# Delta rule's inverse: levels up to 32 rows as 32x32 products of compact diagonal blocks, the last two levels on their non-zero blocks only

## The reference, cut to what matters

```python
def gdn_chunked(q, k, v, g, beta, s0):          # called for both directions
    gcum = jnp.cumsum(chunks(g), axis=-1)
    decay = jnp.where(tri, jnp.exp(gcum_i - gcum_j), 0.0)
    a_mat = jnp.where(strict, (kb @ k.T) * decay, 0.0)       # strictly lower
    t_inv = triangular_solve(eye + a_mat, eye)               # (I + A)^-1
    u, w = t_inv @ (vc * bc), t_inv @ (kb * exp(gcum))
    attn = (q @ k.T) * decay
    def step(state, xs):
        v_new = u_i - w_i @ state
        o_i = q_i @ state + a_i @ v_new
        state = state * exp(gl_i) + k_i.T @ v_new
```

## Time and profile before

| | |
|---|---|
| median of 3 runs | 3282.87 us (3281.56 to 3284.77) |
| the profiled execution | 3282.49 us; its span 3280.6 us |
| delta rule's six steps with lead-in and tail | 340.7 to 706.0 us of the span |
| granted PE clock over the span | 0.928 of 2.4 GHz |

### The profile page before, as it was taken

How to read it: one execution, slowest core, us unless ns; L and a number is a source line. 1 busy time by engine, 2 the same in 40 slices (tenths; PEclk the granted TensorE clock), 3 DMA queues, 4 the chain that set the end, 5 groups by cost and what they waited for, 6 DMA issues and landing times. The chain is left out here.

```text
span 3280.6 us, 39078 instructions
## 1 busy us (share of the span) xinstructions
PE 2813.6 (86%) x15829; PEld 1542.4 (47%) x15829; DVE 912.4 (28%) x1797; ACT 611.6 (19%) x1101; POOL 269.1 (8%) x209
## 2 busy tenths in 40 slices
PE   6998788886999999999889989985698878998993
PEld 4553788863433333444544444432245834444441
DVE  2720455533121121245651000000342554000002
ACT  4411221223101000123221110100232211101002
POOL 0100553421000000000120000000000011000001
PEclk8989899897999999999889999998799988999997
DMA  8122100033799999300147999996401304999996
GB/s 291 52 99 108 65 1 1 14 125 129 321 419 403 416 416 405 114 20 1 65 157 315 430 429 428 429 395 244 160 0 39 134 17 164 423 428 429 429 428 245
DMA packets 109506, 753.39 MB, mean 230 GB/s; under 512 B 20948, under 2 KB 24256, under 8 KB 70480
## 3 DMA queue, kind: packets, MB, share of 16 engines
q1 hardware_dynamic: 106224, 738.19, 54.9%
q0 software_dynamic: 2592, 12.58, 1.0%
q10 hardware_dynamic: 576, 1.05, 0.1%
HBM read 725.82 MB, written 25.97 MB: 229 GB/s over the span
## 5 line engine op out<-in xcount | busy, mean ns | idle before, releaser
L1691 PE MATMUL bank<-ring,expert_in 128*64 128x512 f32 x2048 | 471.4, 615 | 44.4 <-DMA ring<-in_moe_w_up_dram 42.1
L1691 PEld LDWEIGHTS bank<-ring,expert_in 128*64 128x64 f32 x2048 | 162.9, 141 | 346.3 <-issue 343.6
L1702 PE MATMUL bank<-ring,hidden_T 128*64 128x512 f32 x1024 | 226.8, 595 | 41.5 <-ACT hidden_T L1654 40.6
L1630 DVE TENSOR_TENSOR hidden<-silu_gate,bank 128x512 f32<-128x512 f32 x32 | 33.7, 1052 | 749.8 <-PE bank L1691 749.8
L1446 PE MATMUL bank<-ring,expert_in 128*64 128x512 f32 x1024 | 224.8, 597 | 6.5 <-DVE home L1294 5.5
L1680 PEld LDWEIGHTS bank<-onehot,x_part 128*128 128x128 bf16 x3072 | 176.2, 99 | 31.4 <-issue 24.3
L1680 PE MATMUL bank<-onehot,x_part 128*128 128x128 bf16 x3072 | 181.7, 222 | 6.8 <-DVE onehot L1621 6.8
L1702 PEld LDWEIGHTS bank<-ring,hidden_T 128*64 128x64 f32 x1024 | 72.1, 137 | 175.5 <-issue 149.1
L1446 PEld LDWEIGHTS bank<-ring,expert_in 128*64 128x64 f32 x1024 | 73.1, 138 | 156.0 <-issue 141.9
L2386 PE MATMUL bank<-ring,home 128*128 128x512 f32 x256 | 119.2, 628 | 21.6 <-PEq L189 21.6
L547 PE MATMUL bank<-home,ring 128*128 128x512 f32 (+1 forms) x384 | 127.8, 493 | 7.6 <-PEq L189 7.6
(11 more groups left out here) (586 smaller groups left out, 3682.2 us busy)
## 6 DMA issues: line engine op xcount, KB each, us to landing
ring<-in_moe_w_gate_dram SPq DMA_DIRECT2D x67, 2048.0 KB, 17.9
ring<-in_moe_w_up_dram SPq DMA_DIRECT2D x66, 2048.0 KB, 18.5
ring<-in_moe_w_down_dram SPq DMA_DIRECT2D x66, 2048.0 KB, 13.9
ring<-in_w_gate_dram SPq DMA_DIRECT2D x32, 2048.0 KB, 13.2
ring<-in_w_up_dram SPq DMA_DIRECT2D x32, 2048.0 KB, 14.6
ring<-in_w_down_dram SPq DMA_DIRECT2D x32, 2048.0 KB, 16.1
ring<-in_w_mod_dram SPq DMA_DIRECT2D x12, 2048.0 KB, 11.9
expert_rows<-expert_out SPq DMA_DIRECT2D x32, 512.0 KB, 17.4
```

Source lines behind the costliest of these rows:

```text
L1691: mm = pe.matmul(B[2 + 2 * part][rows, :], xe[:, c, rows], ws[e][:, c, :], start=(c == 0), stop=(c == NC - 1))
L1702: mm = pe.matmul(B[6 + b][rows, :], hT[:, c, rows], ws[e][:, c, b * COLS:(b + 1) * COLS], start=(c == 0), stop=(c == NF - 1))
```

## The change

U stays the full 128x128 tile, but for levels 0 to 4 the work is on compact tiles: `Uc`, `Vc`, `ACs`, `ALs`, `Qs` keep the four diagonal 32x32 blocks of each head side by side, 128 partitions by 4x32. A product of a level is then 16 matmuls of 32x32 (4 heads x 4 blocks, block b from partitions 32b to partitions 32b of the result), and the evictions and subtractions are 128x128 in place of 128x512. V is no longer made by a product: DVE transposes `Uc` in 32x32 blocks. All five masks of a step are applied by one POOL operation of 128x640 (`small_masked`), after ACT has cut the diagonal blocks out of A (`cut`, four operations per d). Level 5 multiplies only the 32x32 blocks below (above) the diagonal, level 6 only one 64x64 block per head. Off-diagonal results go straight into U; the diagonal blocks of U are copied there by DVE and ACT (`spread_half`, `spread_rest`). The work for step s+1 is dealt out by direction: one direction per level. `wT` and `vn` get tiles of their own, ring slot 5 holds the compact tiles, and on POOL `prepare` and the clearing of `oacc` come later. The loads on SP are the same.

```diff
+        masks, ALs, ACs = two_small(LS, SM), two_small(LS, HEADS, SM), two_small(HEADS, SM)
+        Uc, Vc, Vq, Qs = two_small(HEADS, SM), two_small(HEADS, SM), two_small(HEADS, 2 * SM), two_small(HEADS, 2 * SM)
...
             def _(pool):
-                pool.memset(oacc[:, :, :], 0.0).then_inc(zeroed, 1)
...
+                def small_masked(s, d):
+                    pool.wait_ge(cut_out, 2 * s + d + 1)
+                    if s:
+                        pool.wait_ge(q_done, step(s - 1, LS - 1, d) + 1)
+                    pool.tensor_tensor(ALs[d], ACs[d].unsqueeze(1).to_broadcast([P, LS, HEADS, SM]),
+                                       masks[d].unsqueeze(2).to_broadcast([P, LS, HEADS, SM]), ALU.mult).then_inc(al_ready, 1)
...
+                def part_of_inverse(s, L, d):
+                    if L == 1:
+                        pe.wait_ge(al_ready, 2 * s + d + 1)
+                    pe.wait_ge(inv_ready, made(s, L - 1, d) + 1)
+                    out = small_bank(d, 0, SM if L <= LS else 2 * SM)
+                    for h in range(HEADS):
+                        if L < LS:
+                            for b in range(P // SM):
+                                mm = pe.matmul(out[blk(b), h, :], ALs[d][blk(b), L, h, :], Uc[d][blk(b), h, :], start=True, stop=True)
+                        elif L == LS:
+                            for p in range(2):
+                                a, b = row_of(d, p), col_of(d, p)
+                                mm = pe.matmul(out[blk(a), h, :], AD[s % 2][d][blk(b), h, blk(a)], Uc[d][blk(b), h, :], start=True, stop=True)
                         else:
+                            a, b = quad(d), quad(1 - d)
+                            mm = pe.matmul(out[a, h, :], AD[s % 2][d][b, h, a], U[d][b, h, b], start=True, stop=True)
+                    mm.then_inc(q_done, 1)
...
+                    for L in range(1, LEVELS):
                         for d in range(2):
+                            part_of_inverse(s, L, d)
+                        if more and L <= 2:
+                            sums_of_gates(s + 1, L - 1)
+                        if more and L in (3, 4):
+                            with_keys(s + 1, L - 3, 4, kk_done)
+                        if more and L >= 5 and s + 1 >= NTC:
+                            with_keys(s + 1, L - 5, 0, qk_done)
+                        for d in range(2):
+                            into_inverse(s, L, d)
...
+                            keep_part(s, L, d)
+                        if L == LS:
+                            for d in range(2):
+                                spread_half(s, d)
+                        if L in (2, 3) and s + 1 < CHUNKS:
+                            exps(s + 1, L - 2)
...
+                    if L < LS:
+                        inv.then(dve.tensor_tensor(Uc[d], Uc[d], small_bank(d, 1), ALU.subtract))
+                        dve.transpose(Vc[d].rearrange("p h f -> p (h f)"), Uc[d].rearrange("p h f -> p (h f)")).then_inc(inv_ready, 1)
```

More of the change, by code:

```diff
@@ L824, in delta_net, with two_small @@
         sq = lambda t, h: idle[:, 14 * W4 + (HEADS * (t % 2) + h) * HD:][:, 0:HD]
+        small = m.ring[:, 5, :]
+        taken_small = [0]
+        def two_small(*shape):
+            size = int(np.prod(shape))
+            out = []
+            for d in range(2):
+                a = small[:, taken_small[0]:taken_small[0] + size]
+                taken_small[0] += size
+                out.append(a.rearrange("p (a b c) -> p a b c", a=shape[0], b=shape[1]) if len(shape) == 3 else a.rearrange("p (a b) -> p a b", a=shape[0]))
+            return out
@@ new lines, in with_keys @@
+                def with_keys(s, d, first, done):
+                    at = AT(chunk_of(s, d))
+                    if first == 4:
+                        pe.wait_ge(exp_ready, 2 * s + d + 1)
+                    else:
+                        pe.wait_ge(kk_taken, 2 * s + d + 1)
+                    for h in range(HEADS):
+                        mm = pe.matmul(pre(d)[:, h * P:(h + 1) * P], qkv[:, 4 + h, at:at + P], qkv[:, first + h, at:at + P],
+                                       start=True, stop=True)
+                    mm.then_inc(done, 1)
@@ new lines, in cut @@
+                def cut(s, d):
+                    act.wait_ge(ad_ready, 2 * s + d + 1)
+                    if s:
+                        act.wait_ge(al_ready, 2 * s + d - 1)
+                    for b in range(P // SM):
+                        ins = act.activation(ACs[d][blk(b), :, :], AD[s % 2][d][blk(b), :, blk(b)], ACT.Copy)
+                    ins.then_inc(cut_out, 1)
+                for d, first in enumerate(("lower0", "upper0")):
+                    at = CONST_NAMES.index(first)
+                    for b in range(P // SM):
+                        act.activation(masks[d][blk(b), :, :], m.const[blk(b), at:at + LS, blk(b)], ACT.Copy).then_inc(tables_made, 1)
@@ L1040, in _ @@
+                for b in range(P // SM):
+                    act.activation(ident[blk(b), :, :], m.c("ident")[blk(b), blk(b)].unsqueeze(1).to_broadcast([SM, HEADS, SM]), ACT.Copy).then_inc(tables_made, 1)
+                for d in range(2):
+                    exps(0, d)
+                for d in range(2):
+                    cut(0, d)
+                act.wait_ge(tables_made, 16)
                 for s in range(CHUNKS):
@@ L1059, in _ @@
                     for d in range(2):
                         act.wait_ge(vn_done, k0 + d + 1)
-                        act.activation(vn[d][:, :, :], bank3(d, 1), ACT.Copy).then_inc(vn_ready, 1)
+                        act.activation(vn[d][:, :, :], heads3(bank(d, 1)[:, :]), ACT.Copy).then_inc(vn_ready, 1)
+                    for d in range(2 if s + 1 < CHUNKS else 0):
+                        cut(s + 1, d)
                 for i, t in enumerate(outer_tiles):
                     act.wait_ge(o_added, i + 3)
-                    squares(t)
+                    for h in range(HEADS):
+                        square(t, h)
@@ L1111, in _ @@
+                for d in range(2):
+                    differences(0, d)
+                for d in range(2):
+                    weights_of_keys(0, d)
+                dve.wait_ge(tables_made, 16)
                 for s in range(CHUNKS):
                     k0 = 2 * s
+                    more = s + 1 < CHUNKS
                     for L in range(LEVELS):
@@ L1129, in _ @@
[L1129 to L1135 removed]
+                                first_level(s, d)
+                            else:
+                                next_level(s, L, d)
+                        if more and L in (1, 2):
+                            differences(s + 1, L - 1)
@@ new lines, in _ @@
+                        if more and L in (4, 5):
+                            weights_of_keys(s + 1, L - 4)
+                        if more and L == 6 and s + 1 >= NTC:
+                            for d in range(2):
+                                dve.wait_ge(ad_ready, 2 * (s + 1) + d + 1)
+                                weights_of_queries(s + 1, d)
+                    if s + 1 == CHUNKS:
+                        dve.wait_ge(o_rooted, 1)
+                        dve.reciprocal(rs[:, inner, :], ms[:, inner, :]).then_inc(o_inverse, 1)
@@ L1148, in _ @@
                                 so.then(ins)
-                        if s + 1 == CHUNKS:
+                        if not more:
                             continue
```

351 lines of the change are left out of this document (177 added, 174 removed).

## The result

| | before | after |
|---|---|---|
| median | 3283.82 us (4 runs, 3281.56 to 3288.28) | 3188.16 us (4 runs, 3185.76 to 3196.33) |
| ratio, 95% interval | | 0.9711 (0.969 to 0.9733) |
| profiled execution, its span | 3282.49, 3280.6 us | 3185.76, 3184.0 us |

What follows compares the result with a forecast made beforehand. PE's throughput, with a short wait over ACT and DVE, was taken to bound the stage. Gains of 14.4 + 19.8 + 67.8 + 20.1 less 0.5 made 121.6 us off 3282.5: 3161 against the median, range 3124 to 3208.

Steps and rivals of the forecast that it cites:

- Group of 16 products: Levels 1 to 4: 32 records of 32x32 products on PE take 0.45 us, 0.55 at half clock.
- fast bound: Lower limit for a group of 32 small records on PE: four blocks at once, 0.22 us.
- Full packing: Rival for the levels: group 0.22 us, clock stays at 2.4 GHz, levels on a 3.0 us floor; 3121 us, chance 0.2.
- slow bound: Upper limit for a group of 32 small records on PE: one record after the other, 0.86 us.
- second rival: Row tiles in the levels don't overlap, group 0.86 us, clock mostly half; 3206 us, chance 0.28.
- Level, 3.2 at full and 4.4 at half clock: Levels 1 to 4 with one direction's inserted work: 3.2 us at full clock, 4.4 at half, mean 3.8 taken.
- Transpose 0.25: In levels 1 to 4, DVE's transpose was taken as 0.25 us, nearest to the 0.22 us copy.
- Boundary 3.1: Between steps, DVE's state update and two small DVE operations: 3.1 us where 5.5 were, 3.6 in step 1.
- Clock 0.6 to 0.85: Granted clock in steps 2 to 4 going to and fro, between 0.6 and 0.85, not 0.92.
- Levels 5 and 6, 4.0 and 4.3: Level 5 with ACT evictions and DVE operations 4.0 us; level 6 with 64x64 products and queries waiting for DVE 4.3.
- Step 5's levels 2.7: Levels of the last step, with nothing inserted for a next step, take 2.7 us each.
- Step 0's stall: PE waits inside level 1 for POOL's `repeat(1)`, behind clearing and `prepare(0)` until 361.2; PE idle some 6 to 8 us.

Runs made afterwards that it cites:

- three edits: Changed kernel with POOL's second-step copies earlier, queries' products behind second halves of levels 5 and 6, first level's subtraction on POOL; together 3159.43 us.
- a fourth: On top of three edits: next gates' products between level 1's first groups, POOL copies ahead of masks, last diagonal copies ahead of the square root; 3167.63 us.

## Why the prediction was right, and where it was off

The sign and the range held, and so did the main mechanism: PE's large products were the bound, and it fell away with them. The sum was 25 us short against the profiled execution (27 by the medians), 22.1 of them in the stage (265.8 against 243.7) and the rest outside it, which is within what executions differ by. Nearly half of the 22 comes from levels 5 and 6, and some from a wait for instructions, a term that the prediction did not have. That it came so near is in part luck: groups that were faster than forecast made up for terms that were too small.

| | before | forecast | measured |
|---|---|---|---|
| lead-in and step 0 | 62.7 | 48.3 | 53.3 |
| step 1 | 55.7 | 35.9 | 39.0 |
| steps 2 to 4 together | 184.2 | 116.4 | 127.0 |
| step 5 to W | 42.8 | 21.2 | 24.4 |
| tail | 19.9 | 21.4 | 22.1 |

- **Group of 16 products, 0.45 us at the full clock and 0.55 at half:** measured 0.26 and 0.42, near the fast bound. Full packing was right and its rival 3121 still wrong. Of the 11 us a step that it misses in steps 2 to 4, 5.4 lie in levels 5 and 6 and 4.1 in levels 1 to 4: those at the full clock do take 3.2, near its 3.0, but those at half clock or with a gap don't. The Trainium skill's rule on one PSUM bank (TensorEngine Tiling (Array Packing), Restrictions and Gotchas) did not hold this group back: four row tiles wrote the bank at 7 ns spacing. The slow bound, 0.86 us, has its like in another order of the same products, 0.64 to 0.72 us at the full clock and 1.0 at half; that kernel takes 3236, where the second rival said 3206.
- **Level, 3.2 at full and 4.4 at half clock, 3.8 taken:** 3.2 to 3.5 and 4.4 to 5.1; four levels of step 2 took 14.9 us where 15.2 were taken. Right in size, by terms that made up for each other. A group takes 0.26, not 0.45, but the second direction comes 0.52 us after the first, behind DVE's subtraction and transpose, and the inserted products take 1.09 us (441.16 to 442.25), not 0.89. From there on PE's order is the way, as forecast.
- **Transpose 0.25:** 0.311 over 48, next to the subtraction's 0.274. The small ACT copies took 0.27 to 0.31 where 0.2 was taken.
- **Boundary 3.1 (3.6 in step 1), and 1.5 more on the wide products:** 3.0 into step 3 (473.77 to 476.72) and 2.9 into steps 4 and 5, but 3.8 into steps 1 and 2; and 12.2 us from W to the last state sum in step 2, as taken (10.7 and 1.5). Right, except for step 2.
- **Clock 0.6 to 0.85:** 0.81 to 0.84 in steps 2 to 4. Right.
- **Levels 5 and 6, 4.0 and 4.3:** the step that failed in steps 1 to 4. They took 4.8 to 5.5 and 5.6: some 2.5 us a step more, near 10 in all. Of the 10.6 us that steps 2 to 4 miss, 7.7 are here; level 3 of step 4, with its gap, is 2.8 more. PE stood 0.7 us behind `weights_of_keys`, and the inserted queries ran, at half clock in level 6, while the second half was ready. Moving them won 6.5 us of the stage.
- **Step 5's levels 2.7:** 3.1 to 3.7. The way over ACT and DVE alone is 2.45, below the forecast, as the run with fewer records shows; the rest is supply, of which the prediction had nothing.
- **Step 0's stall:** it came, 6.5 us of PE ended by POOL's copy at 361.06, as said, and its removal won 7.3 us. Level 4 of that step, taken as 3.0, took 6.4, with a gap of 2.9 us inside a group. It is the same supply; a transfer begins in the gap.
- **DVE as what levels wait for:** named as a way to be wrong; with fewer records the inserted levels stand at 3.1 to 3.4, and what PE's first groups then wait for is DVE's transpose, 0.5 us a level, so it is part of the next bound there.
- **Semaphores cleared at the end, 0.5 us:** no run shows this term by itself; the tail took 22.1 us, 0.7 more than forecast.

Open: how much of the whole is supply and how much clock isn't split. In the levels shown the half clock follows a gap, and a low clock lengthens what comes next. The 10 us by which the stage shrank with fewer records can hold both. What the changed kernel spends in waits for instructions inside levels 1 to 4 is 8.1 us.

## What to carry to other kernels

Count the instructions, not only the columns: when products get small, the supply of PE's instructions becomes a floor (here about 3.4 us for 256 of them, matmul records and weight loads together) and shows as an issue wait inside a group that needs nothing new. To test it, see whether these waits stand 256 instructions apart, or a multiple of that. Lay neighbouring small products on different parts of the array; the same products in the other order cost 50 us. And judge an edit to such a chain by the run: with clock and supply in it, three edits that shortened the stage by 15 us apart shortened it by 24 together, and a fourth that won 2 us in each of two levels lost 7.

## What was not expected of the hardware

- **Supply of instructions.** Transfers of 16 KB, each about 1 us long, followed each other 3.3 to 3.5 us apart at the closest, at the full clock (483.63, 487.06, 490.54) as at half (564.69, 568.01, 571.42); a gap inside a group ended 2.25 to 2.7 us after a transfer had begun. The Trainium skill (Runtime: NRT & Kernel Launch, Instruction fetch mechanics) gives blocks of 16 KiB, 256 instructions, and says that crossing one is mostly hidden. The size agrees with the 250 records per transfer and with gaps at the same place modulo 256; that it is hidden held before (one in 19 us) and not here.
- **DVE beside POOL.** The subtraction L1211, both inputs in SBUF, took 0.28 us where POOL didn't hold it. In eight of its twelve executions a POOL operation that reads SBUF ran already, with more than 0.07 us to go, and it took 0.34 to 1.60 us, ending 0.14 to 0.15 us after that operation each time. Beside a clearing (L931), which reads nothing, it took 0.25. The subtraction L1218, one input in PSUM, and the transpose kept 0.25 to 0.31 beside POOL. Timeline of the boundary to step 2:

```profile
432.18 3.02 POOL L921 TENSOR_TENSOR ring<-ring 128x640 f32<-128x640 f32 x2 [28.80 <-ACT ring L1126]
433.94 1.41 DVE L1211 TENSOR_TENSOR ring<-ring 128x128 f32<-128x128 f32 x1
435.15 1.29 POOL L904 COPY ring<-G 128x512 f32<-128x512 f32 x2
435.39 0.31 DVE L1212 STREAM_TRANSPOSE ring<-ring 128x128 f32<-128x128 f32 x1
```

DVE's operation ends just behind POOL's (435.35 and 435.20), not 0.28 us after its start. By the Trainium skill (SBUF — State Buffer, SBUF: two separate sides) a DVE operation with two SBUF inputs and a GpSimd operation that reads SBUF exclude each other for the whole instruction; the trace agrees, with the clearing as the case that is not held.
- **Pause and clock.** After the pause between steps the first level of steps 1 to 4 ran at 0.50 to 0.66 of the clock and took 4.4 to 5.1 us. With the pause filled by three wide products it ran at 1.00 and took 3.3 to 3.8 us, and the kernel was no faster, since the waits for instructions grew by 5.5 us.
